# Moving the scale, shift and modulation of four layer norms from the Scalar engine to the Vector engine

## The reference

```python
def layer_norm(x, g, b):
    mu = jnp.mean(x, -1, keepdims=True)
    var = jnp.mean(jnp.square(x - mu), -1, keepdims=True)
    return (x - mu) * lax.rsqrt(var + LN_EPS) * g + b

def trunk_layer(h, cond, lp, ...):
    sh1, sc1, g1, sh2, sc2, g2 = jnp.split(silu(cond) @ w_mod + b_mod, 6)   # per stream
    u = h * (1.0 + sc1) + sh1
    m = mixing_sublayer(u, ...)
    h = layer_norm(ALPHA * h + g1 * m, ln1_g, ln1_b)
    u = h * (1.0 + sc2) + sh2
    f = hier_moe(u, lp)
    h = layer_norm(ALPHA * h + g2 * f, ln2_g, ln2_b)
    return h
```

## Time and profile before

| | |
|---|---|
| runs of the kernel before | 1306.6 us median of 3 (1304.43 to 1308.06) |
| profiled execution | 1306.6 us, of which the span from first to last instruction is 1304.8 us |
| PE busy | 1084.2 us, 83% |
| DVE busy | 512.9 us, 39% |
| ACT busy | 320.9 us, 25% |
| POOL busy | 91.7 us, 7% |
| mean granted TensorE clock | 0.912 of full speed |

### The profile page before, as it was taken

How to read it: one execution, slowest core, us unless ns; L and a number is a source line. 1 busy time by engine, 2 the same in 40 slices (tenths; PEclk the granted TensorE clock), 3 DMA queues, 4 the chain that set the end, 5 groups by cost and what they waited for, 6 DMA issues and landing times. The chain is left out here.

```text
span 1304.8 us, 30488 instructions
## 1 busy us (share of the span) xinstructions
PE 1084.2 (83%) x13450; PEld 681.2 (52%) x13450; DVE 512.9 (39%) x1392; ACT 320.9 (25%) x751; POOL 91.7 (7%) x116
## 2 busy tenths in 40 slices
PE   3799987778787977999927999888888977999924
PEld 3456666777775534333314556577885544333312
DVE  0122864254435153322116048646756153322133
ACT  2122044222211051211114321533321051111114
POOL 2200000000000001111020000000000001111000
PEclk9799988999798987999967999989999987999957
DMA  9787561615155333899582124100004523899421
GB/s 360 260 247 265 194 233 48 215 67 196 55 150 179 131 126 107 289 389 368 197 260 59 70 99 99 33 3 3 4 10 146 196 95 103 321 367 383 178 105 48
DMA packets 145250, 217.19 MB, mean 166 GB/s; under 512 B 20691, under 2 KB 104896, under 8 KB 144672
## 3 DMA queue, kind: packets, MB, share of 16 engines
q1 hardware_dynamic: 132256, 179.32, 40.8%
q0 software_dynamic: 9088, 21.97, 4.8%
q10 hardware_dynamic: 3760, 13.77, 2.7%
HBM read 209.65 MB, written 21.10 MB: 177 GB/s over the span
## 5 line engine op out<-in xcount | busy, mean ns | idle before, releaser
L1401 ACT ACTIVATE region<-bank 128x256 f32<-128x256 f32 (+3 forms) x328 | 139.8, 454 | 329.0 <-PE bank L866 105.8
L1285 PE MATMUL bank<-region 128*32 128x512 f32 x1152 | 173.3, 608 | 1.8 <-ACT region L1401 1.7
L2024 DVE COPY_PREDICATED region<-lev,bank 128x512 f32<-128x512 uint8 (+1 forms) x90 | 61.1, 678 | 125.5 <-PE bank L888 125.1
L1057 PE MATMUL bank<-u,ring 128*128 128x384 f32 x320 | 106.5, 488 | 0.0
L1285 PEld LDWEIGHTS bank<-region 128*32 128x32 f32 x1152 | 46.9, 112 | 108.8 <-issue 108.8
L1198 PE MATMUL bank<-u,ring 128*128 128x384 f32 x256 | 86.5, 500 | 5.9 <-DVE u L2107 5.9
L1311 PE MATMUL bank<-ring,region 128*32 128x512 f32 x768 | 87.3, 595 | 1.4 <-ACT region L1401 1.4
L1057 PEld LDWEIGHTS bank<-u,ring 128*128 128x128 f32 x320 | 59.9, 190 | 40.7 <-issue 1.4
L1198 PEld LDWEIGHTS bank<-u,ring 128*128 128x128 f32 x256 | 50.0, 196 | 41.4 <-DVE u L2107 6.3
L1460 ACT ACTIVATE region<-bank 128x384 f32<-128x384 f32 x50 | 23.7, 492 | 183.4 <-PE bank L1057 95.6
L992 PE MATMUL bank<-ring,cond 128*32 128x128 f32 x1536 | 53.2, 290 | 17.7 <-issue 10.7
(11 more groups left out here) (278 smaller groups left out, 1565.6 us busy)
## 6 DMA issues: line engine op xcount, KB each, us to landing
ring<-in_w_mod SPq DMA_DIRECT2D x48, 1024.0 KB
region<-in_moe_w SPq DMA_DIRECT2D x48, 1024.0 KB
ring<-in_moe_w SPq DMA_DIRECT2D x48, 1024.0 KB
ring<-in_w_in SPq DMA_DIRECT2D x20, 768.0 KB
region<-y_rows ACTq DMA_DIRECT2D x6, 1024.0 KB, 9.5
ring<-in_w_in SPq DMA_DIRECT2D x12, 256.0 KB
u_rows<-region ACTq DMA_DIRECT2D x6, 512.0 KB, 2.6
region<-in_bands POOLq DMA_DIRECT2D x2, 1280.0 KB, 7.1
```

The costliest lines, as they stand in the source:

```text
L1057: last = pe.matmul(dst[:, 0:T], w[:, c, tc(m)], u[:, c, :], start=(c == 0), stop=(c == KT - 1))
L1285: last = pe.matmul(bank[p % 2][cols, :], xs[:, p % 2, c, cols], of[(p * P + CTILE * q) // CAP][:, c, :], start=(c == 0), stop=(c == KT - 1))
L1401: return act.activation(dst, src, ACT.Copy)
L2024: dve.copy_predicated(quads(xx_m[:, j, lo:8]), lev[:, k, lo // 2:4, :].unsqueeze(2).broadcast_to([P, 4 - lo // 2, 2, C]), quads(bank[j][:, ...
```

## The change

Norms 0 to 2: the 48 ACT instructions that made `u` are gone, and with them `gain` and the semaphore `xhat_up`. DVE now multiplies a chunk by the norm's scale and by `rstd` in one instruction with two tensor inputs (`stt`), and makes `u` itself in two `ts` instructions per chunk (`normed`), one chunk behind. When all of `u` is made, DVE adds the norm's bias to the 8 chunks of `h`. Norm 3: DVE does the same scaling in 8 instructions and the bias in 8 more; ACT has no part in it. PE turns `h` only when all 8 chunks are final, token tile by token tile instead of chunk by chunk, and ACT copies the banks and starts the output transfers in that order.

```diff
-            for c in range(KT):
-                pe.wait_ge(h_up, KT * (2 * DEPTH - 1) + c + 1)
-                for t in range(NT):
-                    last = pe.transpose(bank[2 * t + c // 4][:, tc(c % 4)], h[:, c, tc(t)], ident)
-                    if c % 4 == 3:
-                        last.then_inc(tail_mm, 1)
+            pe.wait_ge(h_up, KT * 2 * DEPTH)
+            for t in range(NT):
+                for half in range(2):
+                    for q in range(4):
+                        last = pe.transpose(bank[2 * t + half][:, tc(q)], h[:, 4 * half + q, tc(t)], ident)
+                    last.then_inc(tail_mm, 1)
@@ ACT, norm
-                for c in range(KT):
-                    act.wait_ge(xhat_up, KT * n + c + 1)
-                    if n + 1 < 2 * DEPTH:
-                        for g, (lo, hi) in enumerate(STREAMS):
-                            last = act.activation(u[:, c, lo:hi], h[:, c, lo:hi], ACT.Identity,
-                                                  scale=gain[:, c, g:g + 1], bias=shift[:, c, g:g + 1])
-                        last.then_inc(u_up, 1)
-                    else:
-                        act.activation(h[:, c, :], h[:, c, :], ACT.Identity, scale=par[:, l, LN2G + c:LN2G + c + 1],
-                                       bias=par[:, l, LN2B + c:LN2B + c + 1]).then_inc(h_up, 1)
@@ ACT, output
-            for half in range(2):
-                for t in range(NT):
-                    act.wait_ge(tail_mm, NT * half + t + 1)
-                    copy(y_out[:, t, 512 * half:512 * half + 512], bank[2 * t + half][:, :]).then_inc(tail_cp, 1)
-                    if half == 1:
-                        act.wait_ge(tail_cp, NT + t + 1)
+            for g in range(2 * NT):
+                t, half = g // 2, g % 2
+                act.wait_ge(tail_mm, g + 1)
+                copy(y_out[:, t, 512 * half:512 * half + 512], bank[g][:, :]).then_inc(tail_cp, 1)
+                if half == 1:
+                    act.wait_ge(tail_cp, g + 1)
@@ DVE, norm
+                scaled_steps = []
                 for c in range(KT):
-                    tt(h[:, c, :], h[:, c, :], rstd, ALU.mult).then_inc(xhat_up, 1)
+                    scaled_steps.append(mark(stt(h[:, c, :], h[:, c, :], par[:, l, g0 + c:g0 + c + 1], rstd,
+                                                 ALU.mult, ALU.mult)))
+                    if c > 0 and n + 1 < 2 * DEPTH:
+                        after(scaled_steps[c - 1])
+                        normed(c - 1, which)
+                after()
                 if n + 1 < 2 * DEPTH:
-                    for c in range(KT):
-                        dve.wait_ge(u_up, KT * (n + 1) + c + 1)
-                        ts(h[:, c, :], h[:, c, :], par[:, l, g0 + c:g0 + c + 1], par[:, l, b0 + c:b0 + c + 1],
-                           ALU.mult, ALU.add).then_inc(h_up, 1)
-                    dve.wait_ge(h_up, KT * (n + 1))
+                    normed(KT - 1, which)
+                if n + 1 < 2 * DEPTH:
+                    dve.wait_ge(u_up, KT * (n + 2))
+                for c in range(KT):
+                    ts(h[:, c, :], h[:, c, :], par[:, l, b0 + c:b0 + c + 1], None, ALU.add).then_inc(h_up, 1)
+                dve.wait_ge(h_up, KT * (n + 1))
+
+            def normed(c, which):
+                base = 24 * (1 - which)
+                for g, (lo, hi) in enumerate(STREAMS):
+                    last = ts(u[:, c, lo:hi], h[:, c, lo:hi], mod[:, base + 8 + c, g:g + 1], shift[:, c, g:g + 1],
+                              ALU.mult, ALU.add)
+                last.then_inc(u_up, 1)
@@ DVE, shifts
-                g0 = (LN1G, LN2G)[which]
-                link(tt(gain[:, :, :], mod[:, base + 8:base + 16, :],
-                        par[:, l, g0:g0 + KT].unsqueeze(2).broadcast_to([P, KT, 2]), ALU.mult))
```

More of the change, by code:

```diff
@@ L243, in build @@
         shift = sb("shift", [P, KT, 2])
-        gain = sb("gain", [P, KT, 2])
         mod_row = sb("mod_row", [P, P])
@@ L425, in build @@
         gn_c, gn_v, gn_up = sem("gn_c"), sem("gn_v"), sem("gn_up")
-        mixa_up, z_up, xc_up, xhat_up = sem("mixa_up"), sem("z_up"), sem("xc_up"), sem("xhat_up")
+        mixa_up, z_up, xc_up = sem("mixa_up"), sem("z_up"), sem("xc_up")
         d_up, group_up, both_up, pick_up, row_up, plan_up, hid_up, z2_up, h_up = (
@@ L1755, in _ @@
                 norm(l, 1)
-            for half in range(2):
-                for t in range(NT):
-                    act.wait_ge(tail_mm, NT * half + t + 1)
-                    copy(y_out[:, t, 512 * half:512 * half + 512], bank[2 * t + half][:, :]).then_inc(tail_cp, 1)
-                    if half == 1:
-                        act.wait_ge(tail_cp, NT + t + 1)
-                        dst = y_prompt[0] if t == 0 else y_sample[0, (t - 1) * P:t * P]
-                        act.dma_start(dst, y_out[:, t, :]).then_inc(y_out_s, 16)
+            for g in range(2 * NT):
[4 more added lines that the diff above has]
+                    act.wait_ge(tail_cp, g + 1)
+                    dst = y_prompt[0] if t == 0 else y_sample[0, (t - 1) * P:t * P]
+                    act.dma_start(dst, y_out[:, t, :]).then_inc(y_out_s, 16)
         @block.vector
```

## The result

The changed kernel takes 1312.0 us (median of 20 runs), the kernel before 1304.4 us (20 runs on the same chip): ratio 1.0057, 95% interval 1.0039 to 1.0077, in means +7.5 us, give or take 2.2. It is measurably slower, by 0.4 to 0.8%. Forecast were 1310.6 us, a range of 1307.6 to 1313.6, and a step of +4.0 us. The time lies in the range and the kernel is slower, as forecast. The forecast step is too small. The profile of before that I started from (1306.6 us) lay 2.2 us above the median of the later runs, and this hid part of the gap between the two steps.

A forecast was written before the change was run, and what follows sets the result against it. The prediction took PE, busy 83% of the span, to bound the kernel. Its norm terms 0.1 + 0.1 + 0.6 + 3.0 = 3.8 us plus 0.2 for stalls gave +4.0: 1310.6 us from 1306.6, range 1307.6 to 1313.6.

The forecast's parts named there:

- What one DVE instruction costs: DVE in the norms: scalings 0.525 us apart, 0.61 long; pair making a chunk of u 0.575; bias adds 0.332 apart.
- Rival 2: DVE in the norms: alternating instructions don't overlap, a chunk costs 1.36 us; total about +8.5 us, 1315; chance 0.07.
- Norms 0 to 2, the chunks: DVE delivers u every 1.10 us, last at t0 + 8.89; costs +0.1, +0.1 and +0.6 us in norms 0, 1, 2.
- t0: Start of a norm's first scaling on DVE, in the earlier trace 470.40, 706.43, 1055.65 and 1286.20 us.
- The bias behind it: Bias of h after u in norms 0 to 2: takes 2.74 us, covered by 0.4 to 0.6 us in norm 0, cost 0.
- Rival 3: Bias adds run 0.525 us apart and hold up the routing: +0.8 in norms 0 and 2, total +5.6, 1312.2; chance 0.09.
- Norm 3 and the output: Tail: h complete at t0 + 7.07, then transposes mostly at low clock; +3.0 us, bounds +1.6 and +4.9.
- Rival 1: Cheaper tail: early full PE clock, scalings 0.470 us apart; total about +2.5, 1309.1, no measurable change; chance 0.22.
- Rival 4: Router's first products onward: later PE start meets earlier full clock, faster; half the needed size gives 1307; chance 0.07, 0.04 measurably faster.
- +4.0: Whole kernel: forecast step in us, 3.8 from the four norms plus 0.2 for two small stalls; 1310.6 us, +0.31%.
- difference outside the four norms of more than 1 us: Anywhere outside the norms: sign that the forecast is wrong, since none of its terms has such a difference.
- The waits of PE: Expert stage: PE waits for DVE's routing and the sums after the experts, hardly for transfers; last-chunk delays go 1:1 into the end.

The follow-up runs named there:

- e3: Changed kernel with one more 384-element scaling per chunk in norms 0 to 2, spacing the chunks further apart: 1318.1 us, ratio 1.0117 to the kernel before.
- e5: Kernel before with only the new order of transposes, copies and output transfers; norm 3 still scaled on ACT: 1307.9 us (one run), tail 20.20 us.
- e6: Kernel before with only norm 3's scaling and bias moved to DVE, output order as before: 1306.9 us (one run), tail 21.42 us.
- e4: Changed kernel once more, unchanged, measured against the kernel before: 1314.3 us, ratio 1.0071.
- p2: Changed kernel with 16 small idle ACT copies into a spare tile in norms 0 to 2, the tile filling the gap left by gain: 1310.0 us, ratio 1.0053.
- p1: Kernel before with 15 idle DVE writes per layer to a spare tile, moving later tiles up 64 bytes: 1306.6 and 1306.2 us, ratios 1.0021 and 1.0033.
- e7: Kernel before with norm 3's last three chunks on DVE, bank copies split between DVE and ACT, output transfers issued by SP: 1301.5 us, ratio 1.0013.

## Why the forecast was right, and where it fell short

- **What one DVE instruction costs: right.** The new scaling is 0.609 us long (0.61 forecast), a chunk comes every 1.11 us (1.10 forecast), (472.52 - 466.98)/5 between the third scaling and the eighth. Rival 2 is out: its chunk would be 1.35 (0.61 + 0.743, which the prediction rounds to 1.36). e3 found 0.52 to 0.53 for a further scaling (464.40 - 463.88). The Trainium skill (VectorE: DVE Perf Modes, Terms) read strictly has no overlap at all; these distances, shorter than the durations, speak against that reading.
- **Norms 0 to 2, the chunks: right as a sum, in part by luck.** Forecast +0.1, +0.1, +0.6. Read from this pair of traces: norm 0 ends its pass at t0 + 9.90 against 9.92, norm 1 starts 0.16 later, norm 2 ends 0.75 later. Over all traces the old form ends at t0 + 9.15 to 9.93 (16 passes, mean 9.57), the new one at t0 + 9.90 to 9.99 (10 passes, mean 9.92), since DVE and not PE's clock now sets it: +0.35 in each. I had treated the two passes of one trace as two kinds of norm. They were two draws of where the clock returned, and that one was late and one early made their sum, 0.7, come out.
- **The bias behind it: right.** It takes 2.72 us (2.74) and ends 0.37 us before DVE is wanted. Rival 3 is out.
- **Norm 3 and the output: right.** +3.1 for +3.0. PE started at t0 + 7.13 (7.1), at a granted clock of 0.50, the last issue was at t0 + 13.00 (13.0), and the landing took 2.6. Rival 1 is out. e5 and e6 show that its two causes don't add.
- **Rival 4, the clock: no sign of a gain.** The granted mean is 0.914 against 0.912. From t0 to the first expert matmul it is 33.7 to 33.9 us in the old form (mean 33.8) and 33.2 to 35.1 in the new (mean 34.05): the scatter grew, the mean by 0.2. Behind the router's pass of norm 0 the clock even fell again in three traces with the new norms (changed, e4, p2): the 24 transposes of `u` took 4.25 to 4.51 us, at a granted 0.62 and 0.64 in the first two, where every other pass has 2.84. It cost nothing, for just these three reach the first expert matmul at t0 + 33.2.
- **What failed: the line "+4.0" as a whole.** The sum lacked a term, since it took "up to t0 nothing changes" and between the norms as well. I had named a difference outside the four norms of more than 1 us as what would prove me wrong, and this is what happened: 3.5 and 5.8 us more were measured than the norms and the tail hold. In the trace of the changed kernel 1.0 of these are PE's waits for weights and about 2.0 the longer stretch behind the experts of layer 0. The first is in every kernel whose tiles are moved by 64 bytes and in no other, the second in every such kernel and in one other. I had named `gain` falling away as "nothing gained" for its instruction, and never asked what its bytes do to the addresses. What then remains, 0.5 and 3 us, is not explained; the measurements are known to 2.2 and 2.6.
- **The waits of PE: read one step short.** From the earlier trace rows I took it that PE hardly waits for a transfer. But its longest wait there, 22.2 us for L2298, is DVE waiting for ACT, and ACT waiting 18.8 us for the read of `y_rows`:

```profile
674.20 1.15 ACT L1754 ACTIVATE region<-region 128x1024 f32<-128x1024 f32 x1 [18.80 <-DMA region<-y_rows]
```

A transfer does stand behind the experts, and it is this stretch that grew.

One theory fell on the way. In the changed kernel the step from the last copy to the issue of that read took 12.0 us in layer 0, against 9.3 before, and it looked like the missing 3 us. But e4, the same program, took 9.7, and e6, with three norms of before, 12.4. Where the issue falls scatters between executions. The whole stretch up to norm 1 doesn't do so in e4: it is 53.3 us there, too.

The kernels that would settle the tiles' share, before with nothing but a spare tile of 64 bytes, and the changed kernel with it and no idle instructions, were not run. p1 and p2 stand in for them, with instructions added that may cost something of their own.

## What to carry to other kernels

When work moves from one engine to another, work out the pace of the new supplier from start-to-start distances in the trace, not from durations, and compare its last chunk with when the consumer wants it; here this gave each piece to within 0.3 us. When an engine waits for another, ask what that one waited for, until you are at a transfer or at the first cause. Where steps of 0.3% matter, remember that dropping or adding a small tile moves all that come after it: keep the addresses (leave the tile in) when you compare. And run an edit without work beside the real one: here its difference, 3.6 us, was nearly as large as the step that was forecast.

## What the runs showed of the hardware

- The same 132256 packets of one queue take 40.5 to 40.9% or 41.3 to 41.5% of the 16 DMA engines' time, with part of the tiles they fill moved by 64 bytes in either direction. It is the packets of 1024 bytes that take longer, 51.0 to 51.2 ns instead of 48.4 to 48.9.
- One product has its weights 1.5 to 2.0 us ahead of its turn in eight traces. In the six with moved tiles it starts 0.09 us behind their landing, and the pass takes 13.0 to 13.5 us instead of 12.53.
- A PE pass that is fed one chunk every 1.11 us ended at t0 + 9.9 in all ten cases, while the same pass fed faster ended anywhere from 9.15 to 9.93: there the return of the clock from 0.5 to 1 decides, and this differs from one execution to the next.
- Output transfers of the same size landed in 2.6 to 2.9 us when issued 1.5 us apart or more (medians 2.6 and 2.7 in six traces), in 2.6 to 3.7 when 1.0 apart (medians 2.8 to 3.5 in seven), and in 2.7 to 4.1 when all three were issued within 1.1 us (e7, median 3.4).
- An edit that adds no work to any chain, but moves tiles by 64 bytes (p1), measured +3.6 ± 2.2 us (0.28%) over 24 runs.
